# w_ada's forty later tiles, 2.85 units apart in the context's first mixer

## The chip, the cores and the metric

The kernel runs on one core of one Trainium2 chip, in fp32 throughout. The metric is the device time in microseconds, the median of several executions. The core has TensorE (PE), VectorE (DVE), ScalarE (ACT), GpSimd (POOL) and SyncE (SP), which here only issues loads. Each engine works through its own list in order and waits on semaphores.

## The reference, cut to what matters

Two layers work on 256 latent and 256 context tokens of width 1024. In each layer the modulation comes first:

```python
m = jax.nn.silu(cond) @ w + b          # cond: c and c_ctx, w = w_ada[l], 1024 x 6144
sh_a, sc_a, g_a, sh_f, sc_f, g_f = jnp.split(m, 6, axis=-1)
z = split_columns(modulate(x, norm1_gain[l], sh_a, sc_a) @ w_in[l])
mix = jnp.concatenate([pool_x, attn_x, ml_x], axis=-1) @ w_out[l]
x = x + g_a * mix
x = x + g_f * peer_ffn(modulate(x, norm2_gain[l], sh_f, sc_f), ...)
```

The context reads only itself; the latent tokens read themselves and the context. `pool_x` is a centred pooling, `attn_x` low-rank attention with 8 heads, `ml_x` a bidirectional matrix memory with 4 heads. `peer_ffn` picks 16 experts for each of 8 heads of each token out of 16384 and gathers their rows. The context's second layer ends after its keys, values and memory state.

## The kernel before, in words

The work has four mixers (`PHASES`): context layer 0, latent layer 0, context layer 1, latent layer 1. The first and the last run alone; the other two run behind the experts' gathers. This case lies in the first, `mixer(0)`, before any gather.

Each engine's list is written by Python generators that yield a time in units and are merged in order of it (`merge`). Among equal times the generator named first goes first, and the rest tiles' is named ahead of the mixer's. A unit is a place in the order, no duration. In the first mixer the input projection takes 3 units for each of its 16 groups from unit 12 on (`in_at`): 3, 3 and 2 matmuls. The memory stands at 45 (`ALONE_TIMES.ml`), the row products of keys and queries at 60, 64, 70 and 74, their transposes (row turns, L1675) 10 units later, the attention at 87 with 4 units for each of 8 steps, the out-projection at 129.

A step of the attention works on two heads: scores (L1692), VectorE's maxima, ScalarE's exponentials (L902), VectorE's shares, transposes of the probabilities (L1707), ScalarE's copies (L914) and the products with the values (L1722), which VectorE copies out (L1293).

Weights come in tiles of 128 x 2048 fp32 (1024 KB). For the first mixer there are 63 of them (`main_loads`): 8 `ada` tiles of w_ada's shift and scale for the first norm, which must come first; the forty `rest` tiles (16 left of layer 0, `REST_OF[0]`, and 24 of layer 1); 8 `in`, 1 `ukv`, 2 `uq`, 4 `out`. They are sorted by the unit of their first use and go in this order through a ring of five places (`ALONE`). In SyncE's list load n waits until load n - 5 is spent (`spent`: its last matmul done), and every later load stands behind it. An `in` tile serves two groups, 6 units; a `rest` tile is spent at once.

A rest tile (`ada_rest`) is 8 matmuls at L1499 with 32 columns of silu(c) as weights, at unit `rest_at(n)`. Its sum, in `bank[5]`, is copied by ScalarE to `modrow` (L709, unit `rest_at(n) + 1`), and ahead of the next tile TensorE turns it with two small matmuls (L1483, `turn`). After tile 15 VectorE builds `modT` and `A2` of layer 0 (L1048, L1051) at `rest_at(16) - 1`, and tile 16 waits for it; after tile 39 it does the same for layer 1 at `rest_at(40) + 1`. Layer 0's are read from the first out-projection on, layer 1's from the third mixer on.

Other lines that the prediction names: L1534 and L1528 are the input projection, L1506 sums of squares, L1544 and L1554 small transposes of the gates, L1739 the out-projection, L608 the loads of tiles.

Of the kernel before, what the change touches and what calls it, by code (L numbers as in the profile page):

```python
# [48 lines left out]
REST_OF = (ADA_TILES - ADA_FIRST, ADA_TILES)  # L49
# [59 lines left out]

def rest_at(n):  # L110

    return 13 + 2 * n if n < REST_OF[0] else 46 + 2.5 * (n - REST_OF[0])


def n2_at(p):
# [88 lines left out]
def main_loads():  # L204


    def mixer(p):
        at = BASE[p]
        uses = []
        for t in range(IN_TILES):  # L210
            own = [n for n, g in enumerate(groups(p)) if g[2] == t]
            if own:
                uses.append((p, "in", t, at + in_at(own[0]), at + in_at(own[-1]) + 2))
        for what, kinds in (("q", [("uq", 0), ("uq", 1)]), ("k", [("ukv", 0)])):
            rows = [at + row_at(p, j) for j, item in enumerate(items(p)) if item[1] == what]
            if rows:
                uses += [(p, kind, n, rows[0] + n, rows[1] + (n if kind == "uq" else 1)) for kind, n in kinds]
        if PHASES[p][2]:
            for b in range(OUT_TILES):
                first = at + TIMES[p].out + 2 * b * OUT_STEP  # L220
                uses.append((p, "out", b, first, first + OUT_STEP + 2))
        uses.sort(key=lambda u: u[3])
        return uses

    fast = [(0, "ada", j, j - 20, j - 20) for j in range(ADA_FIRST)]
    fast += [(0, "rest", n, rest_at(n), rest_at(n)) for n in range(REST)]
    fast = sorted(fast + mixer(0), key=lambda u: u[3])
    back = mixer(1) + mixer(2)
    last = mixer(3)
    return fast + last[BACK:], back + last[:BACK], len(fast)  # L230
# [91 lines left out]
def build(nc, x_in, c_in, par_in, con_in, w_in, wq_in, uq_in, pw_in, uv_tabs, out):  # L322
    with ExitStack() as ctx:
# [353 lines left out]
        def _(a):  # L677
# [25 lines left out]
            def rest_rows():  # L703
                for n in range(REST):
                    yield rest_at(n) + 1
                    a.wait_ge(rest_mm.sem, rest_mm.at(0, n + 1))
                    if n >= 2:
                        a.wait_ge(rest_tr.sem, rest_tr.at(0, n - 1))
                    a.activation(modrow[:, n % 2, :], bank[5][:, 0:WT], ACT.Copy).then_inc(rest_row.sem, 1)  # L709
# [325 lines left out]
        def _(v):  # L1035
# [21 lines left out]
            def first_scales():  # L1057
                yield 8.5
                v.wait_ge(ada_tr.sem, ada_tr.at(0, ADA_FIRST))
                modulation(0, 0, 16, bank[2], [mix_scale])  # L1060
                v.sem_inc(mod_ready.sem, 1)
                yield rest_at(REST_OF[0]) - 1
                v.wait_ge(rest_tr.sem, rest_tr.at(0, REST_OF[0]))
                modulation(0, 16, 48, bank[5][:, WT - 32:], [ff_scale])
                v.sem_inc(rest_scaled, 1)
                yield rest_at(REST) + 1
                v.wait_ge(rest_tr.sem, rest_tr.at(0, REST))
                modulation(1, 0, 48, bank[5][:, WT + 64:], [mix_scale, ff_scale])
                v.sem_inc(mod_ready.sem, 1)
# [897 lines left out]
```

## Time and profile before

| what | value |
|---|---|
| runs | 2668.5, 2670.63, 2673.1 us; median 2670.63 |
| the profiled execution's own time | span 2664.6 us from its first to its last instruction; no other total is recorded for it |
| TensorE busy | 2150.9 us, 81% of the span |
| VectorE, ScalarE, GpSimd busy | 1636.1, 1140.6, 810.0 us |
| mean granted TensorE clock | 0.949 |
| DMA | 940.05 MB, mean 353 GB/s |
| chain that ended last | DMA 45%, PE 33%, DVE 10%, ACT 7%, issue 3% |
| first mixer's out-projection begins | 251.45 us |

A busy share is an average over stages with different limits. From about 340 us on gathers fill the DMA engines for most of the span; the first mixer lies ahead of that, so it must be read by itself, in windows and in the timeline. In the timeline an fp32 matmul has two records, so "x16" is eight matmuls.

### The profile page before, as it was taken

What the parts mean: (1) busy time and instruction counts of PE and PEld (TensorE: products, weight loads), DVE (VectorE), ACT (ScalarE), POOL (GpSimd) and SP (SyncE); (2) the same over time, 40 slices, a digit from 0 to 9 for tenths busy, and PEclk for the clock granted to TensorE, in tenths of its full rate; (3) what the DMA queues carried; (4) which work ended last, traced back from release to release, by engine and by line L of the source; (5) the groups of instructions that cost most, each with busy time, mean ns of one, the idle gap of its engine ahead of it and who ended that gap; (6) DMA issues with size and microseconds to landing.
All of it is one profiled execution on the core that took longest, in us unless ns stands there. A gap on an engine that the chain in (4) does not pass through costs nothing.

```text
span 2664.6 us, 26635 instructions
## 1 busy us (share of the span) xinstructions
PE 2150.9 (81%) x8372; PEld 1003.3 (38%) x8372; DVE 1636.1 (61%) x4029; ACT 1140.6 (43%) x3280; POOL 810.0 (30%) x772
## 2 busy tenths in 40 slices
PE   6899889876788677796677777789989987777776
PEld 3667745432344243351122111166774321221111
DVE  1125376687887665766677666445536666677654
ACT  3144264555774434455333333335423333443332
POOL 0000033443445334333434333200004444343331
PEclk8999999978999889998899999999899999999999
DMA  7667199999999999999999999922019999999997
GB/s 302 255 247 316 34 397 412 396 362 392 407 399 405 421 414 412 418 419 421 422 421 422 421 422 421 412 89 76 36 34 392 425 426 426 425 426 426 426 426 308
DMA packets 133660, 940.05 MB, mean 353 GB/s; under 512 B 14864, under 2 KB 16144, under 8 KB 23312
## 3 DMA queue, kind: packets, MB, share of 16 engines
q0 software_dynamic: 110592, 805.36, 73.0%
q1 hardware_dynamic: 22496, 130.31, 12.4%
q10 hardware_dynamic: 432, 2.70, 0.3%
q8 instruction: 66, 1.08, 0.2%
q14 instruction: 74, 0.61, 0.1%
HBM read 937.26 MB, written 1.05 MB: 352 GB/s over the span
## 4 chain that ended last, share of the span: by engine, by line
DMA 45%; PE 33%; DVE 10%; ACT 7%; issue 3%; POOL 1%; SPq 0%; DVEq 0%; POOLq 0%; ACTq 0%
DMA fast<-uv_dram,idx 27%; DMA mix<-uv_dram,idx 14%; PE bank L1816 11%; PE bank L1775 5%; PE bank L1534 4%; DVE fast L1400 4%; PE bank L1739 2%; DMA qring<-wq_dram 2%; DMA fast<-w_dram 2%; PE bank L1499 2%; PE bank L1528 1%; PE bank L1784 1%; ACT diag L973 1%; ACT coef L970 1%; PE bank L1506 1%
## 5 line engine op out<-in xcount | busy, mean ns | idle before, releaser
L1816 PE MATMUL bank<-fast,diag 128*64 128x512 f32 x1956 | 797.0, 653 | 247.4 <-ACT diag L973 242.5
L667 POOL DMA_INDIRECT fast<-uv_dram,idx x489 | 525.8, 1075 | 1395.0 <-PE bank L1816 695.1
L1400 DVE SCALAR_TENSOR_TENSOR fast<-fast,hrow 128x1024 f32<-128x1024 f32 x489 | 598.3, 1224 | 347.9 <-DMA fast<-uv_dram,idx 342.2
L969 ACT ACTIVATE gact<-araw 128x1 f32<-128x1 f32 x768 | 154.5, 201 | 904.3 <-DVE fast L1400 548.2
L1816 PE MATMUL bank<-mix,diag 128*64 128x512 f32 x816 | 387.4, 628 | 99.3 <-ACT diag L973 96.5
L1816 PEld LDWEIGHTS bank<-fast,diag 128*64 128x64 f32 x1956 | 190.5, 144 | 706.6 <-ACT diag L973 454.3
L1400 DVE SCALAR_TENSOR_TENSOR mix<-mix,hrow 128x1024 f32<-128x1024 f32 x204 | 250.0, 1226 | 178.3 <-DMA mix<-uv_dram,idx 174.0
L667 POOL DMA_INDIRECT mix<-uv_dram,idx x204 | 203.4, 997 | 291.7 <-PE bank L1816 270.2
L973 ACT ACTIVATE diag<-con,coef 128x64 f32<-128x64 f32 x768 | 267.1, 348 | 25.1
L970 ACT ACTIVATE coef<-gact,wts 128x1 f32<-128x1 f32 x768 | 226.2, 295 | 24.9
L1816 PEld LDWEIGHTS bank<-mix,diag 128*64 128x64 f32 x816 | 93.2, 139 | 341.2 <-ACT diag L973 224.7
L1775 PE MATMUL bank<-hT,qring 128*128 128x256 f32 x640 | 192.0, 421 | 32.7 <-DMA qring<-wq_dram 24.0
L1775 PEld LDWEIGHTS bank<-hT,qring 128*128 128x128 f32 x640 | 115.0, 199 | 145.9 <-issue 103.6
L1816 PE MATMUL bank<-hT,diag 128*64 128x512 f32 x224 | 114.7, 637 | 41.0 <-ACT diag L973 40.3
L1400 DVE SCALAR_TENSOR_TENSOR hT<-hT,hrow 128x1024 f32<-128x1024 f32 x56 | 68.6, 1224 | 41.2 <-DMA hT<-uv_dram,idx 41.2
L1534 PE MATMUL bank<-hT,back 128*128 128x256 f32 (+1 forms) x336 | 84.1, 390 | 4.0 <-ACT hT L716 4.0
L667 POOL DMA_INDIRECT hT<-uv_dram,idx x56 | 56.6, 1011 | 95.5 <-PE bank L1816 92.8
L1534 PE MATMUL bank<-hT,fast 128*128 128x256 f32 (+1 forms) x320 | 81.3, 407 | 4.8 <-ACT hT L716 4.8
L1816 PEld LDWEIGHTS bank<-hT,diag 128*64 128x64 f32 x224 | 27.3, 142 | 115.7 <-ACT diag L973 76.6
L1534 PEld LDWEIGHTS bank<-hT,fast 128*128 128x128 f32 (+1 forms) x320 | 62.1, 200 | 22.7 <-issue 13.2
L1534 PEld LDWEIGHTS bank<-hT,back 128*128 128x128 f32 (+1 forms) x336 | 63.4, 191 | 18.0 <-issue 7.4
L969 ACT ACT_TABLE_LOAD x53 | 68.0, 1283 | 0.9
(265 smaller groups left out, 2588.6 us busy)
## 6 DMA issues: line engine op xcount, KB each, us to landing
fast<-w_dram SPq DMA_DIRECT2D x72, 1024.0 KB, 8.9
qring<-wq_dram SPq DMA_DIRECT2D x40, 576.0 KB
back<-w_dram SPq DMA_DIRECT2D x20, 1024.0 KB
fast<-uv_dram,idx POOLq DMA_INDIRECT x489
mix<-wq_dram SPq DMA_DIRECT2D x8, 576.0 KB, 5.6
mix<-uv_dram,idx POOLq DMA_INDIRECT x204, 27.5
fast<-uq_dram SPq DMA_DIRECT2D x4, 576.0 KB, 3.8
xT<-x_dram ACTq DMA_DIRECT2D x1, 2048.0 KB, 8.6
```

The source lines that it names most:

```text
L667: g.indirect_dma_start(slot(e, m), None, uv_tabs[e], bass.IndirectOffsetOnAxis(idx[:, Q % 2, n:n + 1], 0)).then_inc(landed[place], 16)
L969: link(a.activation(gact[:, n:n + 1], araw[:, Q % 2, n:n + 1], ACT.Gelu))
L970: link(a.activation(coef[:, n:n + 1], gact[:, n:n + 1], ACT.Copy, scale=wts[:, Q % 2, n:n + 1]))
L973: a.activation(diag[:, m % DIAGS, :], two, ACT.Copy, scale=coef[:, n:n + 1]).then_inc(diag_ready.sem, 1)
L1400: v.scalar_tensor_tensor(out=u, in0=u, scalar=1.0, in1=hrow[:, (2 * i + half) % 3, :], op0=ALU.mult, op1=ALU.mult, accum_out=araw[:, Q % 2 ...
L1499: mm = t_.matmul(bank[5][strip(k), 0:WT], cS[:, k, :], w[:, k, :], start=(k < STRIPS), stop=(k >= KC - STRIPS))
L1506: t_.matmul(bank[3][:, 0:SEQ], ones, sq[:, n % 2, :], start=first, stop=last).then_inc(sq_used.sem, 1)
L1528: mm = t_.matmul(bank[g % 2][:, 0:WT], own_h(p)[:, k, n * P:(n + 1) * P], w[:, k, :], start=(k == 0), stop=(k == KC - 1))
L1534: mm = t_.matmul(bank[g % 2][0:rows, 0:SEQ], w[:, k, o:o + rows], own_h(p)[:, k, :], start=(k == 0), stop=(k == KC - 1))
L1739: mm = t_.matmul(bank[b % 2][:, 0:SEQ], w[:, k, b % 2 * P:b % 2 * P + P], own_h(p)[:, k, :], start=(k == 0), stop=(k == KC - 1))
L1775: mm = t_.matmul(dst[:, 0:SEQ], query_tile(e, u)[:, k, :], own_h(p)[:, k, :], start=(k == 0), stop=(k == KC - 1))
L1816: mm = t_.matmul(acc[half, f * 512:(f + 1) * 512], diag[:, j % DIAGS, :], slot(e, j)[:, D + f * 512:D + (f + 1) * 512], start=(j % SLOTS < ...
```

## The change

The spacing of the forty rest tiles is one line. Before, tiles 0 to 15 stood at units 13 to 43, 2 apart, and tiles 16 to 39 at units 46 to 103.5, 2.5 apart. Now all stand 2.85 apart, from 13 to 124.15. What hangs on `rest_at` moves along: copies, turns, VectorE's two modulations (from unit 45 to 57.6 and from 107 to 128), and the place of each tile in the order of loads. No instruction is added or removed.

```diff
 def rest_at(n):
 
-    return 13 + 2 * n if n < REST_OF[0] else 46 + 2.5 * (n - REST_OF[0])
+    return 13 + 2.85 * n
```

The order of loads around the in tiles, as tile (unit of first use), from load 8 on:

before: in 0 (12), rest 0 (13), 1 (15), 2 (17), in 1 (18), rest 3 (19), 4 (21), 5 (23), in 2 (24), rest 6 (25), 7 (27), 8 (29), in 3 (30), rest 9 (31), 10 (33), 11 (35), in 6 (36), rest 12 (37), 13 (39), 14 (41), in 5 (42), rest 15 (43)

now: in 0 (12), rest 0 (13), 1 (15.85), in 1 (18), rest 2 (18.7), 3 (21.55), in 2 (24), rest 4 (24.4), 5 (27.25), in 3 (30), rest 6 (30.1), 7 (32.95), 8 (35.8), in 6 (36), rest 9 (38.65), 10 (41.5), in 5 (42), rest 11 (44.35), 12 (47.2), in 4 (48), rest 13 (50.05)

First place: SyncE's list, from the loads that wait for an ada tile on. `in_mm` is the semaphore of a spent in tile, `rest_mm` of a spent rest tile, `ada_mm` of a spent ada tile. Before:

```order
L608 DMA fast<-w_dram 128x2048 [waits ada_mm] x8
L608 DMA fast<-w_dram 128x2048 [waits in_mm]
L608 DMA fast<-w_dram 128x2048 [waits rest_mm] x3
L608 DMA fast<-w_dram 128x2048 [waits in_mm]
L608 DMA fast<-w_dram 128x2048 [waits rest_mm] x3
L608 DMA fast<-w_dram 128x2048 [waits in_mm]
```

Now:

```order
L608 DMA fast<-w_dram 128x2048 [waits ada_mm] x8
L608 DMA fast<-w_dram 128x2048 [waits in_mm]
L608 DMA fast<-w_dram 128x2048 [waits rest_mm] x2
L608 DMA fast<-w_dram 128x2048 [waits in_mm]
L608 DMA fast<-w_dram 128x2048 [waits rest_mm] x2
L608 DMA fast<-w_dram 128x2048 [waits in_mm]
```

Three loads that wait for rest tiles stood between two that wait for an in tile; now two do here (three once, later).

Second place: TensorE's list from the second or third rest tile on, beside in tiles 0 and 1 and the start of in tile 2. Before:

```order
L1499 MATMUL bank<-fast,cS 32x256 x8
L1534 MATMUL bank<-hT,fast 128x256 x2
L1544 MATMUL bank<-con,mix 128x32 x2
L1534 MATMUL bank<-hT,fast 128x256 x3
L1483 MATMUL bank<-con,keysA 128x2 x2
L1499 MATMUL bank<-fast,cS 32x256 x8
L1534 MATMUL bank<-hT,fast 128x256 x5
L1483 MATMUL bank<-con,keysA 128x2 x2
L1499 MATMUL bank<-fast,cS 32x256 x8
L1534 MATMUL bank<-hT,fast 128x256 x6
L1483 MATMUL bank<-con,keysA 128x2 x2
L1499 MATMUL bank<-fast,cS 32x256 x8
```

Now:

```order
L1499 MATMUL bank<-fast,cS 32x256 x8
L1534 MATMUL bank<-hT,fast 128x256 x8
L1483 MATMUL bank<-con,keysA 128x2 x2
L1499 MATMUL bank<-fast,cS 32x256 x8
L1534 MATMUL bank<-hT,fast 128x256 x8
L1506 MATMUL bank<-mix,con 128x256 x2
L1483 MATMUL bank<-con,keysA 128x2 x2
L1499 MATMUL bank<-fast,cS 32x256 x8
```

Between two tiles (L1499) stood 5 or 6 projection matmuls (L1534); now 8 do.

Third place: TensorE's list from the last two steps of the attention to the out-projection (L1739). Before:

```order
L1722 MATMUL bank<-hrow,mix 64x128 x2
L1707 MATMUL bank<-con,hrow 128x128 x2
L1722 MATMUL bank<-hrow,mix 64x128 x2
L1707 MATMUL bank<-con,hrow 128x128 x2
L1722 MATMUL bank<-hrow,mix 64x128 x2
L1707 MATMUL bank<-con,hrow 128x128 x2
L1722 MATMUL bank<-hrow,mix 64x128 x4
L1739 MATMUL bank<-hT,fast 128x256 x19
```

Now:

```order
L1483 MATMUL bank<-con,keysA 128x2 x2
L1499 MATMUL bank<-fast,cS 32x256 x8
L1707 MATMUL bank<-con,hrow 128x128 x2
L1722 MATMUL bank<-hrow,mix 64x128 x4
L1483 MATMUL bank<-con,keysA 128x2 x2
L1499 MATMUL bank<-fast,cS 32x256 x8
L1483 MATMUL bank<-con,keysA 128x2 x2
L1739 MATMUL bank<-hT,fast 128x256 x19
```

Rest tiles with their turns now stand between the last transposes, and the last turn directly ahead of the out-projection.

## Rows read from the trace of the kernel before

**Rows 1.** Waits of TensorE, 0 to 300: us in total, times, longest us.
```profile
PE bank L1499 <- DMA fast<-w_dram: 15.3, 5, 3.5
```

**Rows 2.** Waits of the load queue, 0 to 300: us in total, times, longest us.
```profile
SPq L608 <- PE bank L1534: 86.6, 6, 18.6
```

**Rows 3.** Chain of waits, 55 to 135: start us, us, what.
```profile
58.29 4.83 DMA fast<-w_dram
...
91.51 4.76 DMA fast<-w_dram
...
124.55 5.01 DMA fast<-w_dram
```

**Rows 4.** TensorE's timeline: start, us, operation, records, in brackets idle before.
```profile
63.17 1.94 PE L1499 MATMUL bank<-fast,cS 128*32 128x256 f32 x16 [2.84 <-DMA fast<-w_dram]
65.03 4.48 PE L1534 MATMUL bank<-hT,fast 128*128 128x256 f32 x10
...
80.99 1.07 PE L1499 MATMUL bank<-fast,cS 128*32 128x256 f32 x16 [2.44 <-DMA fast<-w_dram]
...
86.22 2.86 PE L1534 MATMUL bank<-hT,fast 128*128 128x256 f32 x12
88.92 0.50 PE L1483 MATMUL bank<-con,keysA 128*128 128x2 f32 x4
89.35 1.07 PE L1499 MATMUL bank<-fast,cS 128*32 128x256 f32 x16
90.35 2.43 PE L1534 MATMUL bank<-hT,fast 128*128 128x256 f32 x10
...
96.32 1.77 PE L1499 MATMUL bank<-fast,cS 128*32 128x256 f32 x16 [3.20 <-DMA fast<-w_dram]
98.02 3.37 PE L1534 MATMUL bank<-hT,fast 128*128 128x256 f32 x10
...
112.92 1.32 PE L1499 MATMUL bank<-fast,cS 128*32 128x256 f32 x16 [3.38 <-DMA fast<-w_dram]
114.18 3.81 PE L1534 MATMUL bank<-hT,fast 128*128 128x256 f32 x10
...
129.61 1.07 PE L1499 MATMUL bank<-fast,cS 128*32 128x256 f32 x16 [3.45 <-DMA fast<-w_dram]
130.61 4.11 PE L1528 MATMUL bank<-fast,hT 128*128 128x256 f32 x10
```

**Rows 5.** Windows: stretch, busy us of each engine (records), clock, DMA share, GB/s.
```profile
62.50:69.50 7.00, 6.33 (x29) 4.20 (x29) 2.21 (x6) 0.38 (x1) 0.00 (x0) 0.52 1.02 430
...
134.50:212.00 77.50, 76.75 (x553) 51.68 (x552) 27.20 (x51) 40.58 (x83) 0.00 (x0) 0.98 0.69 272
```

**Rows 6.** Timelines of TensorE (204.16, 209.16) and VectorE (201.38), row phase.
```profile
204.16 1.08 PE L1675 MATMUL bank<-con,hrow 128*96 128x128 f32 x8
...
209.16 1.94 PE L1499 MATMUL bank<-fast,cS 128*32 128x256 f32 x16
...
201.38 0.96 DVE L1253 TENSOR_TENSOR hrow<-hrow,par 128x768 f32<-128x768 f32 x1
```

**Rows 7.** TensorE's timeline, attention to out-projection.
```profile
222.97 1.13 PE L1692 MATMUL bank<-mix,fast 96*128 96x256 f32 x4
...
229.96 1.16 PE L1692 MATMUL bank<-mix,fast 96*128 96x256 f32 x4 [0.91 <-ACT hrow L902]
...
238.36 0.61 PE L1483 MATMUL bank<-con,keysA 128*128 128x2 f32 x4 [0.17 <-ACT keysA L709]
...
239.75 1.13 PE L1692 MATMUL bank<-mix,fast 96*128 96x256 f32 x4
...
242.65 1.13 PE L1692 MATMUL bank<-mix,fast 96*128 96x256 f32 x4
...
251.45 4.80 PE L1739 MATMUL bank<-hT,fast 128*128 128x256 f32 x21 [0.38 <-DVE hT L1293]
```

**Rows 8.** Groups by line, 0 to 300: busy us, mean ns, idle before.
```profile
L709 ACT ACTIVATE keysA<-bank 128x256 f32<-128x256 f32 x40 | 15.3, 382 | 64.9 <-PE bank L1499 64.7
```

## The prediction

> **What bounds the kernel now.** I read the waits of TensorE and of the load queue first, over the stretch that the change touches (the start to 300 us). TensorE waits 15.3 us in five pieces for weight tiles at L1499, the matmuls of w_ada's later tiles [rows 1]. The load queue's largest wait is 86.6 us, for L1534, the in-projection [rows 2]: a load stands still until a projection tile is spent, and all loads behind it stand too. The chain of waits shows each case as one piece, "DMA fast<-w_dram": there are five, of 4.76 to 5.01 us from issue to landing, and every one begins in the moment an in-projection tile is spent [rows 3]. The timeline of TensorE then shows what a wait costs: the idle time in brackets, and slower matmuls behind it [rows 4]. The table of windows shows the granted clock and the transfer rate after the first wait, and that from 134.5 to 212 us TensorE is busy 76.75 of 77.5 us [rows 5]. So this mixer is bound by TensorE, except for five holes in which it waits for a tile.
>
> Why the holes are there. The five places of the ring are refilled in order of use, so the load of number n waits for number n-5. An in tile is held for 6 units. With rest tiles 2 units apart, three stand between two in tiles, and the tile that reuses an in tile's place is a rest tile due 2 units after the in tile is spent: rest 3 after in 0 (19 against 17), rest 6 after in 1 (25 against 23), rest 9 after in 2, rest 12 after in 3, rest 15 after in 6. In 2 units TensorE has under 2.5 us of work, and the load takes 4.8. That gives exactly the five waits of the trace. After rest 16 the distance of 2.5 units gives no sixth.
>
> **The change part by part.** Nothing is added or removed: 40 tiles, each with 8 matmuls, a turn of 2 matmuls, a copy on ScalarE and a load of 1 MB. Units of work at full clock, from [rows 4]: six projection matmuls take 88.92 - 86.22 = 2.70 us, so 0.45 each; a turn (L1483) 89.35 - 88.92 = 0.43; a tile 90.35 - 89.35 = 1.00. (A matmul is two records.)
>
> First, the five idle stretches. They are 2.84, 2.44, 3.20, 3.38 and 3.45 us, sum 15.3. With 2.85 units between rest tiles, the tile that reuses an in tile's place comes later. The work between the last matmul on the in tile and the wait for the new one becomes:
> in 0 to rest 3: 3 matmuls, turn and tile, 8 matmuls, turn: 11 x 0.45 + 1.43 + 0.43 = 6.8 us;
> in 1 to rest 5: the same 6.8 us and the two small groups L1506 and L1554;
> in 2 to rest 7: 8 matmuls, turn and tile, turn: 3.60 + 1.43 + 0.43 = 5.46 us;
> in 3 to rest 9: 5.46 us;
> in 6 to rest 12: 16 matmuls, two tiles with turns, turn: 7.2 + 2.86 + 0.43 = 10.5 us.
> Loads land 4.76 to 5.01 us after issue when nothing is queued ahead [rows 3]. A tile of 1.05 MB takes 1.05 / 0.43 = 2.44 us of transfer at the 430 GB/s of [rows 5]. Each of the first releases sends out three loads, of which the third lands after 4.8 + 2 x 2.44 = 9.7 us, and the next release comes after 16 matmuls and two tiles with turns, 7.2 + 2.86 = 10.1 us: nothing is queued ahead of the next burst. Only ahead of rest 12 is one more load, and there 10.5 us are free. The places of the later in tiles, of ukv and of uq are wanted again 4 units and more after their release, as from rest 16 on before, where nothing waited. So all five waits go: -15.3 us, with 0.45 us to spare at two places.
>
> Here the Trainium skill speaks against the change: "DMA: Bandwidth & Descriptors", section Specifications, gives about 358 GB/s as a core's limit from HBM. By it a tile takes 2.93 us, a load about 5.3, and the two tight places would have 0.15 us left. The trace does not agree: it shows 430 GB/s.
>
> Second, the clock behind the holes. The stretch from 62.5 to 69.5 has a granted clock of 0.52 [rows 5], so half of it and more ran at 1.2 GHz where full is 2.4. Row by row against the full-speed row (five projection matmuls in 2.43, a tile in 1.07) [rows 4]: first wait 4.48 - 2.43 = 2.05 and 1.94 - 1.07 = 0.87; second nothing; third 0.94 and 0.70; fourth 1.38 and 0.25; fifth 1.68. Sum 7.9 us. I take all of it back, since each slow piece follows an idle stretch of 2.8 us or more and no other piece between 48 and 134 is slow. Bounds: 0, if the clock falls without a wait too, as at 209.16, where a tile took 1.94 us with no idle time in front [rows 6]; and 7.9 + 0.9 = 8.8, if that one goes as well.
> By the Trainium skill, "TensorE: Matmul & The Clock Gate", section HAM oscillation, it is waits for DMA between bursts that bring the half rate again and again. By that rule alone the whole 7.9 would come back; the row at 209.16 does not agree with it as the only cause.
>
> Third, the moved tiles. Before, rest 0 to 32 (33 tiles) stand ahead of the attention (unit 87); after, rest 0 to 25. Seven tiles go behind the fourth step's scores (unit 99): -7 x 1.43 = -10.0 us there, +10.0 us here, if TensorE is the bound at both ends. Ahead, what the other engines must deliver stays in time: the closest is the row turn at 204.16, whose rows VectorE finished at 201.38 + 0.96 = 202.34 [rows 6], 1.8 us early, and two tiles stand between its last row product and it before and after alike. In the attention, a step without a tile is 242.65 - 239.75 = 2.90 us [rows 7]; the small waits between scores, turns and values in it can take up a little of a tile. The step from 222.97 to 229.96 lasts 6.99 us with two tiles, 2.90 + 2.86 = 5.76 of it work: there VectorE and ScalarE hold TensorE, but this place has three tiles around it before and after. I take 7 x 0.1 = 0.7 us of gain (bounds 0 and 1.5). At the end the last tile and its turn now stand right ahead of the out-projection, and the turn waits for ScalarE's copy, 0.38 us [rows 8] and a hand-over each way, 0.6 us; in exchange the 0.38 us wait at 251.45 [rows 7] is covered: +0.2 us. VectorE's modulation for layer 1 moves there as well and is needed only in the latent tokens' later phase; the out tiles' loads follow rest 35 to 38 and have over 5 us before their use.
>
> Sum: -15.3 - 7.9 - 0.7 + 0.2 = -23.7 us. All that follows (queries, gathers, later mixers) starts when this mixer ends and has no other clock, so it moves as a whole. Against the profiled span: 2664.6 - 23.7 = 2640.9. The median of the runs shown is 6.0 us over that span, so 2670.6 - 23.7 = 2646.9 us.
>
> **The rivals.**
> A, the two tight places still wait. For: 0.45 us to spare is little, and loads spread by 0.25 us. Against: every landing of the trace is below 5.1. Price from the nearest case, one more tile queued ahead: 4.8 + 2.44 - 5.46 = 1.8 us each, and with it a slow piece of 7.9 / 5 = 1.6 each: 6.8 us less gain, 2653.7 us.
> B, the clock falls anyway. For: the row at 209.16. Against: the long stretch 134.5 to 212 is at 0.98 with no waits. The 7.9 us stay: 2654.8 us.
> C, the change only shifts the holes: the load that reuses an in tile's place is late whatever the distance, and five waits stay. Against: rest 18, 20 and 22 of before, 4 and more units behind their release, wait for nothing. 2670.6 us.
> D, slower: the attention cannot take the tiles. Nine tiles now stand between unit 99 and 129, each with a turn that waits for ScalarE, whose copy may stand behind an exponential that waits for VectorE. If each of the nine waited out a whole step of 2.90 us, that is 26.1 us against the 23.7 gained: 2673.0 us, slower; it decides from 2.6 us a tile. Against: the turn at 238.36, the only one that waited, did so for 0.17 us [rows 7].
>
> **How the numbers follow.** My forecast 0.64, A 0.14, B 0.12, C 0.05, D 0.05. A and B together would be 2661. The range leaves out about 2 in 10: it goes from 2641 (the slow piece at 209 gone, the attention at its best, and 3 us of scatter as the three runs have) to 2658 (A or B with scatter). No change means within 0.2%, 5.3 us, about what a measurement of this kernel can tell. Faster: forecast, A, B and a little of C, 0.91; same 0.05; slower 0.04.
>
> **What would show it.** The waits for "DMA fast<-w_dram" at L1499 between 50 and 135 us gone, or under 1 us in sum; the out-projection's first matmul at about 228 in place of 251.45; granted clock near 1.0 in the stretch from 50 to 110; the tile's matmuls in every step of the attention, steps of 4.3 us and more where they were 2.9; one wait of some 0.6 us ahead of L1739. Two waits of 1 to 2 us would be A, projection rows of 3 to 4 us with no idle time ahead B. A wait of over 1 us at L1483 in the attention would make me wrong in D's direction.

## The result and the profile after

The changed kernel takes 2653.11 us (median of 4 runs, 2651.11 to 2655.41) against 2671.56 us (median of 4 runs on the same chip, 2668.5 to 2673.1): a ratio of 0.9928, 95% interval 0.9915 to 0.9941. That is 18.5 us less, where 23.7 were forecast. A second timing of the same code, below as e_same, gives 0.9916 (0.9903 to 0.9928), 23.2 us less than its own runs of before. The two intervals overlap, and a gain of some 21 us (a ratio of 0.992) lies within both; I take it as the size.

First the waits of TensorE from 0 to 300 us, after (us in total, times, longest us), to be read against [rows 1].

```profile
PE bank L1473 <- DMA fast<-w_dram: 15.3, 2, 14.7
PE bank L1534 <- ACT hT L716: 4.8, 1, 4.8
...
PE bank L1692 <- ACT fast L888: 1.2, 1, 1.2
...
PE bank L1692 <- ACT hrow L902: 0.9, 1, 0.9
...
PE bank L1483 <- ACT keysA L709: 0.7, 2, 0.5
```

The row of L1499, five times and 15.3 us, is gone. The waits at L1473 at the kernel's start are 15.3 us in all, where they were 16.3. New is one of 1.2 us at the first scores (L1692) for ScalarE's L888, the copy of the last row turn.

The load queue's waits, after, in the same columns, against [rows 2]:

```profile
SPq L608 <- PE bank L1534: 64.2, 6, 17.3
SPq L608 <- PE bank L1499: 54.1, 21, 4.5
```

The queue still stands most of the time: loads go out when places come free, and now most of them are freed by later tiles instead of projection tiles. That costs nothing, since TensorE waits for none of it.

TensorE's timeline after, on the stretch that answers to the first wait of [rows 4] (start us, us, operation, records, in brackets the idle time before):

```profile
60.40 1.07 PE L1499 MATMUL bank<-fast,cS 128*32 128x256 f32 x16
61.40 3.72 PE L1534 MATMUL bank<-hT,fast 128*128 128x256 f32 x16
64.95 0.50 PE L1483 MATMUL bank<-con,keysA 128*128 128x2 f32 x4
65.39 1.07 PE L1499 MATMUL bank<-fast,cS 128*32 128x256 f32 x16
```

No brackets, a tile in 1.07 us and sixteen projection records in 3.72: all at full rate. Two windows after (stretch, busy us of PE, PEld, DVE, ACT, POOL with records, granted clock, DMA share, GB/s), and the same two before:

```profile
46.00:130.00 84.00, 83.40 (x582) 63.51 (x586) 20.03 (x47) 27.95 (x60) 0.00 (x0) 0.97 0.65 253
150.00:229.00 79.00, 76.14 (x663) 50.81 (x662) 39.95 (x112) 42.32 (x110) 0.00 (x0) 1.00 0.85 319
```

```profile
46.00:130.00 84.00, 68.68 (x483) 50.04 (x485) 15.92 (x37) 20.89 (x46) 0.00 (x0) 0.90 0.56 220
150.00:229.00 79.00, 78.15 (x610) 52.81 (x608) 33.42 (x73) 44.84 (x96) 0.00 (x0) 0.98 0.78 315
```

In the first 84 us TensorE is now busy 83.40 instead of 68.68 and the clock is 0.97 instead of 0.90. Last, the attention and the out-projection after, against [rows 7]:

```profile
181.49 1.10 PE L1692 MATMUL bank<-mix,fast 96*128 96x256 f32 x4 [1.17 <-ACT fast L888]
...
202.11 1.13 PE L1692 MATMUL bank<-mix,fast 96*128 96x256 f32 x4
...
206.46 1.13 PE L1692 MATMUL bank<-mix,fast 96*128 96x256 f32 x4
...
210.04 0.61 PE L1483 MATMUL bank<-con,keysA 128*128 128x2 f32 x4 [0.17 <-ACT keysA L709]
...
228.90 0.61 PE L1483 MATMUL bank<-con,keysA 128*128 128x2 f32 x4 [0.50 <-ACT keysA L709]
229.37 2.84 PE L1739 MATMUL bank<-hT,fast 128*128 128x256 f32 x12
```

A step of the attention with a tile lasts 206.46 - 202.11 = 4.35 us, the 2.90 + 1.43 of the working. The out-projection starts at 229.37, 22.1 us earlier than at 251.45.

Where the profiled spans' difference of 15.3 us (2664.6 to 2649.3) lies, from the first row of each operation in the two timelines:

| stretch | before | after | difference |
|---|---|---|---|
| start to the first in-projection (L1534) | 45.2 | 46.6 | +1.4 |
| from there to the first scores (L1692) | 168.9 | 134.9 | -34.0 |
| scores to out-projection (L1739) | 37.3 | 47.9 | +10.6 |
| queries, gathers, mixers 1 and 2, layer 0's experts, to the last expert product at 1737.9 and 1716.0 | 1486.4 | 1486.6 | +0.2 |
| to layer 1's first query (1956.64 and 1940.26) | 218.8 | 224.3 | +5.5 |
| to the end | 708.0 | 709.0 | +1.0 |

The first mixer is 23.4 us shorter. The lead is still 21.9 us at 1716.0, and then the last mixer, which the change doesn't touch, gives back 5.5.

### The profile page after: what moved, and what is told of

Same layout as the page of the kernel before. It is cut to its first block, busy times and chain, and to the rows that moved or that the text cites. A ratio compares the mean times of both kernels' runs of the same rounds, so it can differ in the third digit from the quotient of the medians.

```text
span 2649.3 us, 26635 instructions
## 1 busy us (share of the span) xinstructions
PE 2151.9 (81%) x8372; PEld 1004.5 (38%) x8372; DVE 1636.5 (62%) x4029; ACT 1138.7 (43%) x3280; POOL 814.6 (31%) x772
## 3 DMA queue, kind: packets, MB, share of 16 engines
q8 instruction: 66, 1.08, 0.2%
## 4 chain that ended last, share of the span: by engine, by line
DMA 44%; PE 34%; DVE 9%; ACT 7%; issue 3%; POOL 1%; another core or an unknown queue 0%; SPq 0%; DVEq 0%; POOLq 0%; ACTq 0%
DMA fast<-uv_dram,idx 26%; DMA mix<-uv_dram,idx 15%; PE bank L1816 11%; PE bank L1775 4%; PE bank L1534 4%; DVE fast L1400 3%; PE bank L1739 2%; DMA qring<-wq_dram 2%; PE bank L1528 1%; PE bank L1499 1%; PE bank L1784 1%; ACT diag L973 1%; ACT coef L970 1%; PE bank L1506 1%; PE bank L1623 1%
## 5 line engine op out<-in xcount | busy, mean ns | idle before, releaser
L1775 PE MATMUL bank<-hT,qring 128*128 128x256 f32 x640 | 192.8, 423 | 35.0 <-DMA qring<-wq_dram 23.7
L1534 PE MATMUL bank<-hT,back 128*128 128x256 f32 (+1 forms) x336 | 84.5, 391 | 4.0 <-ACT hT L716 4.0
L1534 PE MATMUL bank<-hT,fast 128*128 128x256 f32 (+1 forms) x320 | 75.7, 390 | 4.8 <-ACT hT L716 4.8
L939 ACT ACTIVATE pq<-bank 128x256 f32<-128x256 f32 x48 | 18.2, 380 | 125.6 <-PE bank L1775 116.1
L1534 PEld LDWEIGHTS bank<-hT,back 128*128 128x128 f32 (+1 forms) x336 | 63.9, 192 | 18.3 <-issue 7.4
```

Source lines behind the costliest of these rows:

```text
L1534: mm = t_.matmul(bank[g % 2][0:rows, 0:SEQ], w[:, k, o:o + rows], own_h(p)[:, k, :], start=(k == 0), stop=(k == KC - 1))
L1775: mm = t_.matmul(dst[:, 0:SEQ], query_tile(e, u)[:, k, :], own_h(p)[:, k, :], start=(k == 0), stop=(k == KC - 1))
```

## The experiments

Unless said otherwise, each kernel is the changed one with the one line in rest_at changed. The 40 tiles are numbered n = 0 to 39, and REST_OF[0] is 16. "Out" is the start of the first L1739.

**e_same, the change again.**

```
+    return 13 + 2.85 * n
```

> The changed kernel once more, to see what of its result repeats. Both profiles so far agree that the first mixer's out-projection begins 22 us earlier (251.45 to 229.37) and that layer 0's last expert product starts 21.9 us earlier; 6.2 us of it are lost in the last mixer, between 1738 and 2000 us, whose code is untouched and whose granted clock was lower. Theory (scatter of the clock): the first mixer repeats within 2 us, the last mixer comes out anywhere between 258 and 270 us, and the time is 16 to 22 us under before. Rival (the change itself slows the last mixer): its length is again 268 to 270 us.

Measured: 2650.25 us (5 runs) against 2673.43 (20 runs); ratio 0.9916 (0.9903 to 0.9928); out at 229.58. These 20 runs of before also serve the next three. From the first in-projection to the out-projection it takes 182.9 us, after 182.8, so the first mixer repeats. The stretch of the last mixer that took 218.8 us before and 224.3 after takes 221.2 us here: between the two, as scatter would have it. The gain of 23.2 us is a little over the 16 to 22 expected.

**e_late_only, only the later 24 tiles spread.**

```
-    return 13 + 2.85 * n
+    return 13 + 2 * n if n < REST_OF[0] else 46 + 3.25 * (n - REST_OF[0])
```

> Tiles 0 to 15 stay 2 units apart, tiles 16 to 39 stand 3.25 apart up to 120.75: the move of tiles into the attention without the wider spacing in front. Theory (ring waits): the five waits for w_dram at L1499 stay, 14 to 16 us in sum, the out-projection begins at 251 +-2, time within 0.2% of before. Rival (the gain comes from moving tiles out of the stretch ahead of the attention into its gaps): no less than 8 us faster.

Measured: 2672.96 us (12 runs), ratio 1.0 (0.9991 to 1.001), out at 251.84. Its waits of TensorE, 0 to 300 us:

```profile
PE bank L1499 <- DMA fast<-w_dram: 15.3, 5, 3.3
```

The five waits are untouched, and tiles moved from ahead of the attention into it gain nothing by themselves: the stretch to the scores is 6.4 us shorter (162.5), the attention 6.3 longer (43.6). So the gain hangs on the first sixteen.

**e_front_only, the first sixteen at 2.85, the rest squeezed to end about where they did.**

```
-    return 13 + 2.85 * n
+    return 13 + 2.85 * n if n < REST_OF[0] else 58.6 + 1.975 * (n - REST_OF[0])
```

> Tiles 0 to 15 stand 2.85 apart, tiles 16 to 39 closer, 1.975 apart, so that the last stands before unit 106 as in the kernel before. Theory: all five waits are gone, no new wait of over 1 us for w_dram, out-projection at 228 to 231, time 16 to 22 us under before, like the whole change. Rival (moved tiles): under half of the change's gain, 10 us or less.

Measured: 2660.24 us (9 runs), ratio 0.9953 (0.9938 to 0.9968), out only at 248.22. The expectation missed. The waits of TensorE, 0 to 300 us, are few:

```profile
PE bank L1483 <- ACT keysA L709: 3.1, 4, 1.5
PE bank L1499 <- DMA fast<-w_dram: 2.7, 2, 1.9
```

Together they are 5.8 us, yet the out-projection is 18.8 us behind that of after. (The profiled execution, span 2663.6, was a slower one than the median; the runs put the loss against e_same at 10 us.) The timeline shows half-rate rows in two kinds of place:

```profile
158.58 1.93 PE L1499 MATMUL bank<-fast,cS 128*32 128x256 f32 x16 [1.88 <-DMA fast<-w_dram]
...
191.79 1.94 PE L1675 MATMUL bank<-con,hrow 128*96 128x128 f32 x8
```

The first stands right behind waits of 0.53 and 1.88 us, the second has only one of 0.79 us ahead of it, over 3 us earlier. The windows show what they cost, here of e_front_only (columns as above):

```profile
160.00:180.00 20.00, 20.00 (x116) 12.03 (x108) 6.77 (x13) 9.91 (x19) 0.00 (x0) 0.81 0.55 220
180.00:200.00 20.00, 18.60 (x159) 12.22 (x158) 7.05 (x13) 9.34 (x20) 0.00 (x0) 0.79 1.01 412
200.00:228.00 28.00, 26.46 (x190) 17.95 (x193) 13.24 (x41) 11.86 (x33) 0.00 (x0) 0.73 0.82 303
```

and of after:

```profile
160.00:180.00 20.00, 20.00 (x170) 13.85 (x168) 9.19 (x16) 12.90 (x26) 0.00 (x0) 1.00 0.86 338
180.00:200.00 20.00, 17.83 (x170) 12.42 (x162) 13.94 (x43) 12.18 (x33) 0.00 (x0) 1.00 0.94 364
200.00:228.00 28.00, 27.81 (x262) 18.24 (x264) 10.73 (x43) 11.07 (x40) 0.00 (x0) 1.00 0.83 292
```

From 160 to 180 both are busy for the whole 20 us, but one finishes 170 records and the other 116, at a clock of 0.81. From 180 to 200 the changed kernel idles more (2.17 against 1.40 us) and keeps the full clock. So more idle time is not what costs here; the clock is. The expectation had nothing for it.

**e_two_waits, the first seven tiles still 2 units apart.**

```
-    return 13 + 2.85 * n
+    return 13 + 2 * n if n < 7 else 25 + 2.85 * (n - 6)
```

> Tiles 0 to 6 stand 2 apart, all others 2.85: of the five places where a load waits for an in tile, the first two keep their distance of 2 units. Theory: exactly two waits for w_dram at L1499 stay, at tiles 3 and 6, 4.8 to 5.5 us in sum, with the slow matmuls behind them (2.9 us by the rows of before), so the out-projection begins some 8 us later than in the changed kernel, at 236 to 239, and the time is about 11 us under before. Rival (any wider mean spacing brings the gain, the single place does not matter): as fast as the changed kernel within 2 us.

Measured: 2656.8 us (6 runs), ratio 0.9947 (0.9934 to 0.9961), out at 236.99. Its timeline of TensorE has two waits for tiles:

```profile
64.48 1.56 PE L1499 MATMUL bank<-fast,cS 128*32 128x256 f32 x16 [2.87 <-DMA fast<-w_dram]
80.99 1.07 PE L1499 MATMUL bank<-fast,cS 128*32 128x256 f32 x16 [2.41 <-DMA fast<-w_dram]
```

Two waits of 5.3 us are back, and behind each a slow piece: tile and projection behind the first take 1.6 us more than at full rate, the projection and a small transpose behind the second 1.6 too. The out-projection comes 7.4 us later than in e_same and the kernel takes 6.6 us more. But this profile's in-projection began 1.35 us earlier (45.36 and 46.71), ahead of anything that differs; counted from there the out-projection comes 8.8 us later, 5.3 for the waits and 3.2 for the clock behind them, close to the 4.8 to 5.5 and the 2.9 expected. Waits come back singly, exactly where a place of the ring is wanted too early.

**e_one_wait, tiles 17 and 18 earlier by 2.6 and 4.3 units.** It asks whether a wait alone brings the slow clock of e_front_only.

```
-    return 13 + 2.85 * n
+    return {17: 58.9, 18: 60.01}.get(n, 13 + 2.85 * n)
```

> The changed kernel, but tiles 17 and 18 stand at units 58.9 and 60.01 instead of 61.45 and 64.3, so that tile 18, whose load waits for in 7 (spent at 59), is wanted one unit later. It asks why the run with only the front tiles spread lost 16 us with just 2.7 us of waits for tiles: its granted clock fell to half in three stretches after 158 us. Theory W (one wait of 1 to 2 us at this place, between small matmuls, brings the slow stretches): a wait of 1 to 1.5 us at tile 18 near 141 us, slow stretches of 10 us and more behind it in the first mixer, the out-projection 5 us or more later than the changed kernel's 229.4. Theory D (tiles close together in the stretch of row products and turns, units 60 to 106, bring it: 24 there against 16): the same wait, and the out-projection at 231 to 233, no slow stretch after 60 us.

Measured: 2650.81 us (6 runs) against 2671.64 (11 runs, which serve this and the next three), ratio 0.9928 (0.9909 to 0.9947), out at 230.03. The row of TensorE's timeline:

```profile
145.78 1.07 PE L1499 MATMUL bank<-fast,cS 128*32 128x256 f32 x16 [1.25 <-DMA fast<-w_dram]
```

A wait of 1.25 us, and the tile behind it at full rate; the clock stays at 1.00 in every window from 140 to 228. Counted from the first in-projection the out-projection comes 1.6 us later than in e_same, for this wait and 0.7 us of others at the turns (L1483): no clock was lost. The wait is shorter than the 0.53 and 1.88 us ahead of the first slow piece of e_front_only, so it leaves open what brought that piece.

**e_uniform_26, all tiles 2.6 units apart.**

```
-    return 13 + 2.85 * n
+    return 13 + 2.6 * n
```

> All tiles 2.6 apart, the last at unit 114.4. By the arithmetic of the ring no load is late (the closest has the same 5.5 us as in the changed kernel), so by the theory that only the waits count it is as fast as the changed kernel: no wait over 0.5 us for w_dram, 18 to 24 us under before. The turn that stood bare ahead of the out-projection is covered, 0.5 us. If tile density costs clock (theory D), 18 tiles stand in units 60 to 106 against 16, and a slow stretch of 3.4 us may be there, 1.7 us. Rival: the value 2.85 itself matters, and 2.6 is over 5 us slower.

Measured: 2652.69 us (6 runs), ratio 0.9931 (0.991 to 0.9951), out at 229.12: no difference from the change that can be told. One wait for a tile is there, 0.96 us at 106.63, where none over 0.5 was expected: between release and use lie 5.3 us, and this load took 6.22 from issue to landing (100.36 to 106.58 in the chain of waits). So a place with half a us to spare can fail; why this landing was late isn't shown. Another wait is of 1.54 us for ScalarE's copy at 198.83, and behind it a tile and a scores row run at half rate, 1.6 us lost. So 2.85 is not a special number.

**e_early_two and e_early_three, the first two or three tiles ahead of the in-projection.** TensorE waits 4.8 us there for hT in all other kernels; these fill the hole.

```
-    return 13 + 2.85 * n
+    return 8.1 + 0.1 * n if n < 2 else 13 + 2.85 * (n - 1)
...
-                    yield rest_at(n) + 1
+                    yield rest_at(n) + (0.5 if n < 2 else 1)
```

(and with 3 and n - 2 in the other)

> Tiles 0 and 1 move to units 8.1 and 8.2, ahead of the input projection, where TensorE of both kernels waits 4.8 us for the normed rows; their copies move to 0.5 behind, ahead of the modulation on ScalarE; all later tiles keep 2.85 and end 2.85 units earlier. Theory: two tiles with turns, 2.9 us, go into the 4.8 us wait, which falls to about 1.5 us with the hand-overs to ScalarE, and with less idle time the slow stretch behind it (44.3 to 51.1 us in the changed kernel, 3.4 us of cost) may go. 2.9 to 6 us faster than the changed kernel, out-projection at 223 to 227. Rival: the copies on ScalarE delay the modulation, and it is no faster.

> The same with three tiles at 8.1 to 8.3. Each takes 1.0 us of matmuls, some 0.6 for the copy and hand-overs and 0.4 for its turn, so three are 6 us against the 4.8 us wait. Theory: the third gains at most its turn and tile (1.4 us) and delays the modulation on ScalarE by up to 1.3 us: within 1.5 us of the kernel with two. Rival (TensorE's work alone counts): 1.4 us faster than with two.

Measured: e_early_two 2643.85 us (6 runs), ratio 0.9904 (0.9887 to 0.992), out at 226.22; e_early_three 2648.28 (6 runs), 0.9914 (0.9898 to 0.993). TensorE's timeline after, at the start of the in-projection:

```profile
46.60 2.85 PE L1534 MATMUL bank<-hT,fast 128*96 128x256 f32 x6 [4.79 <-ACT hT L716]
49.38 1.70 PE L1499 MATMUL bank<-fast,cS 128*32 128x256 f32 x16
```

and that of e_early_two, from the end of the work ahead of it:

```profile
41.67 1.07 PE L1499 MATMUL bank<-fast,cS 128*32 128x256 f32 x16
43.25 0.61 PE L1483 MATMUL bank<-con,keysA 128*128 128x2 f32 x4 [0.50 <-ACT keysA L709]
43.78 1.81 PE L1499 MATMUL bank<-fast,cS 128*32 128x256 f32 x16
46.65 7.01 PE L1534 MATMUL bank<-hT,fast 128*96 128x256 f32 x22 [1.06 <-ACT hT L716]
```

The in-projection starts at the same time, and two tiles are done by then. Out comes 3.2 us earlier than after, as expected; the slow stretch at the start of the projection, which might have gone, stays (clock 0.83 from 40 to 60 in both). It has the lowest median of all, 6.4 us under e_same and 7.0 under e_one_wait; the intervals of the ratios overlap, so that it beats the change by time is likely rather than shown, that it beats before is shown. The third tile starts the projection 0.9 us later (47.51) and adds a turn that waits 0.50 us: out comes 0.2 us earlier than with two, no further gain to speak of. Its median is 4.4 us above that of e_early_two, more than the 1.5 expected; the first mixer doesn't show them, and the intervals overlap.

**e_dense, as the change up to tile 21, the rest 1.7 units apart.** It asks for the slow clock of e_front_only without a wait for a tile.

```
-    return 13 + 2.85 * n
+    return 13 + 2.85 * n if n < 22 else 75.7 + 1.7 * (n - 22)
```

> Tiles 0 to 21 as in the changed kernel, tiles 22 to 39 stand 1.7 apart from unit 75.7 to 104.6, behind the last projection weights, so that many tiles stand between small matmuls but no load has to be late. 23 tiles stand in units 60 to 106, as many as in the run with only the front tiles spread (23), against 18 in the kernel before and 16 in the changed one. Theory D (density of tiles, whose matmuls have 32 columns of weights, between row turns and memory products brings the low clock): one or more slow stretches between 165 and 225 us, 10 us or more in sum, out-projection at 235 or later, 5 us or more slower than the changed kernel. Theory W (it was the wait for a tile): waits for w_dram under 0.5 us, clock 1.0, out-projection at 229 to 231.

Measured: 2662.04 us (5 runs) against 2671.89 (9 runs), ratio 0.9965 (0.9952 to 0.9979), out at 237.47, 8 us later than the change. Its windows (columns as above), and its timeline of TensorE:

```profile
140.00:165.00 25.00, 25.00 (x166) 14.88 (x166) 13.75 (x23) 15.44 (x34) 0.00 (x0) 1.00 0.74 296
165.00:200.00 35.00, 34.50 (x338) 23.92 (x340) 16.35 (x42) 19.25 (x44) 0.00 (x0) 0.95 0.98 401
200.00:237.00 37.00, 34.33 (x226) 21.97 (x218) 15.55 (x57) 14.48 (x47) 0.00 (x0) 0.77 0.73 278
```

```profile
177.71 0.61 PE L1483 MATMUL bank<-con,keysA 128*128 128x2 f32 x4
178.25 1.65 PE L1499 MATMUL bank<-fast,cS 128*32 128x256 f32 x16
179.82 1.94 PE L1675 MATMUL bank<-con,hrow 128*96 128x128 f32 x8
...
203.21 1.02 PE L1483 MATMUL bank<-con,keysA 128*128 128x2 f32 x4 [2.48 <-ACT keysA L709]
204.16 1.93 PE L1499 MATMUL bank<-fast,cS 128*32 128x256 f32 x16
206.02 0.69 PE L1707 MATMUL bank<-con,hrow 128*128 128x128 f32 x2
206.64 1.12 PE L1722 MATMUL bank<-hrow,mix 128*64 128x128 f32 x4
207.68 2.08 PE L1692 MATMUL bank<-mix,fast 96*128 96x256 f32 x4
```

No wait for a tile is left, and the half clock is there: from the tile at 178.25 on, with no idle time in front since 140 (25.00 of 25 us busy; of the next 35 only 0.50 are idle, at 183.79, behind it), and from about 203 for some 17 us. The first piece costs 1.7 us. This second piece stands behind a wait of 2.48 us, so for it, the larger one, density and wait are not told apart.

**e_before_again and e_before_third, the kernel before, profiled twice more.** They ask whether the 5.5 us lost in the last mixer belong to the change.

> The kernel before once more, for the last mixer: from layer 0's last expert product to layer 1's first query it took 218.8 us in the profile of before, 220.1 to 225.1 us in nine profiles of kernels with other rest tiles, whose code there is the same. Theory (scatter): 219 to 225 here too, and out-projection of the first mixer at 251 to 252. Rival (the spread of the rest tiles costs something in the last mixer): 217 to 220.

> The same once more, a third profile of the kernel before, with the same two expectations: 219 to 225 us by scatter, 217 to 220 if the spread tiles cost something there.

Measured: one run each, 2674.7 and 2677.46 us, spans 2672.9 and 2675.7. The last mixer from layer 0's last expert product to the first query, as windows of the first profile of before, of e_before_again, and of after:

```profile
1737.90:1956.60 218.70, 198.47 (x948) 154.79 (x946) 98.98 (x231) 94.69 (x198) 0.00 (x0) 0.93 0.17 60
```

```profile
1738.60:1963.60 225.00, 203.62 (x948) 158.50 (x946) 99.49 (x231) 94.82 (x198) 0.00 (x0) 0.90 0.16 58
```

```profile
1716.00:1940.30 224.30, 202.92 (x949) 157.91 (x947) 99.58 (x231) 94.88 (x198) 0.00 (x0) 0.90 0.16 59
```

The same 948 records take 198.47 us at a clock of 0.93 or 203.62 at 0.90, in one and the same kernel. Over the 13 profiles of this study the stretch lasts 218.8 to 225.1 us, and the shortest is that of the first profile of before, the one that the prediction was read from. So the last mixer came out as scatter would have it (225.0 and 224.7 us). The first did not: its out-projection begins at 252.8 and 248.6, where 251 to 252 were expected.

## Why the prediction was right, and where its sizes were off

The forecast was 2647 us with a range of 2641 to 2658; the time is 2653.11, and 2650.25 in the second timing. The mechanism held: the five waits and the slow rows behind them were the cost, and both are gone. One step did not hold, that the other engines deliver in time ahead of the attention, and three sizes were off.

*The five idle stretches, -15.3.* Right. All five are gone, also at the places with 0.45 us to spare, ahead of tiles 7 and 9, which start at 81.76 and 90.45 without a bracket. Rival A (two tight places still wait) and C (the holes only shift) fall with that, though A's fear had a ground: in e_uniform_26 a load took 6.22 us and was waited for. e_two_waits puts two waits back by position alone, and e_late_only all five, with no gain left: the waits are shown as the source.

*The clock behind the holes, -7.9.* Right in kind, sized too low. To the scores the stretch is 34.0 us shorter. Summed from start to start in the two timelines, idle time falls by 13.9 us (the five waits of 15.3 gone, 1.2 us new at the first scores and 0.2 elsewhere), tiles and turns by 12.7, projection rows by 6.5 and row turns by 0.7. Seven tiles moved away are some 10.4 of the 12.7, so 9.5 us are left for the clock, above the upper bound of 8.8. The bound counted 0.9 us for the slow piece at 209.16 and left out its second row:

```profile
211.02 1.82 PE L1675 MATMUL bank<-con,hrow 128*96 128x128 f32 x8
```

At full rate that row takes 1.08 us [rows 6], so the piece cost 1.6 us. It is gone as well: the clock is 1.00 from 150 to 229. Rival B (the clock falls anyway) falls for this kernel. But its ground was sound: in e_dense the half clock at 179.82 has no idle time in front. Nor is the clock's price fixed: in e_before_third the same five waits (14.7 us) cost 6.4 us of slow rows where they cost 7.9, behind the last, of 3.15 us, all rows are at full rate, and nothing is slow near 209. Of the kernels with the later tiles 2.85 or 3.25 units apart, none has a slow piece between 150 and 226; at 2.6 and 2.5 units there is one of some 3 us (at 199.36 in e_uniform_26, 209.16 in before) in all but that one profile of before; at 1.975 and 1.7 it is about 20 us or more. So the slow pieces go with the close spacing, in four kernels; which feature of it brings them no run tells.

*The moved tiles, -0.7.* Here a step failed: "what the other engines must deliver stays in time". At 181.49 the first scores wait 1.17 us for ScalarE's L888, and the chain of waits after (start us, us, what) shows what held ScalarE:

```profile
177.38 1.28 ACT L823
...
179.09 1.29 ACT mix L823 x3
180.41 0.35 issue
180.77 0.59 ACT fast L888
```

A table load and four of the memory's exponentials (L823) stand ahead of the copy; before, ScalarE had done them and waited 0.61 us for TensorE (at 212.15). The wait is there in every kernel with the later tiles 2.85 or 3.25 apart, and in none of the closer ones. In the attention itself there was no gain either: it took 10.6 us more, where 10.0 less 0.7 and the 0.2 of the last turn make 9.5. By the same sums seven tiles are 7.1 of it and their turns 3.7, 0.52 us each among the small products where 0.43 were reckoned; idle time was 1.5 us before and 1.6 after, so the steps had no holes for tiles to fill.

What I undersold is the spacing of the later tiles. By my sum their move was worth 0.7 us; e_front_only, without it, lost 10 us against e_same (2660.24 to 2650.25), mostly to the clock. Still, that kernel squeezes them to 1.975 units, below the 2.5 of before; no run has the first tiles spread and the later ones at 2.5, and e_uniform_26, with 2.6 throughout, lost nothing that can be told.

*The last turn, +0.2.* Right: 0.50 us of wait at 228.90 in place of the 0.38 at 251.45. Rival D (the attention can't take the tiles) falls: the turns in it wait 0.17 us in all up to that last one.

*"All that follows moves as a whole."* Right for the work in this pair: 22.08 us of lead at the first products with the experts' keys (L1784, 331.68 to 309.60) and 21.9 at 1716.0. The last mixer's clock then hid 5.5 us of it, and the repeats show that this is scatter. The stretch between scatters too: from the out-projection to the last expert product e_before_third took 7.0 us more than before.

*The sum* of the first mixer came out to 0.3 us (-23.4 for -23.7), and that is in part luck: 1.6 us too little for the clock stood against 1.2 us for the new wait and 1.1 for the attention. The out-projection's lead is only 22.1 us, as the in-projection began 1.4 us later in this profile.

*The frame* was "the median of the runs shown is 6.0 us over that span". In every run with both figures the time is about 1.8 us over its span (2651.11 and 2649.3), so by my estimate the profiled execution took about 2666.4, 4.2 us under that median: a short one. Repeats of the same kernel have spans of 2672.9 and 2675.7, 8 and 11 us more. Out-projection starts of the changed kernel at 229.37 and 229.58 against 251.45, 252.8 and 248.6 of the three profiles of before give a lead of 19 to 23 us, 21.5 in the mean. The gains of 18.5 and 23.2 us by the medians lie on both sides of that; 23.7 was a little high.

Left open: how much of the half clock behind 203 in e_dense its one wait of 2.48 us brings, what besides the close spacing a slow piece without idle time needs, and whether e_early_two is faster than the change by more than its intervals tell.

## What to carry to other kernels

In a ring of loads that is refilled in order, write for each load which place it waits for, and compare the work between that place's release and the new tile's use with one landing (here 4.8 us, once 6.2): here the places that fell short cost their idle time and about half as much again in clock. Even spacing over the whole stage cured it; closing up the tiles in one part to spread them in another brought the half clock back, in part without any wait. An engine that sped-up work now catches up with must be looked at too: here ScalarE, 1.2 us. Before a sum is set against a profiled span, look how far repeated profiles of the same kernel lie apart, here 11 us of 2665.

## What the runs showed of the hardware

- The granted clock can fall to half without idle time in front. In e_dense TensorE was busy 25.00 of 25 and 34.50 of 35 us when the row at 179.82 took 1.94 us instead of 1.08 [rows 6]. Waits of 0.96 and 1.25 us (e_uniform_26, e_one_wait) had full-speed rows behind them, one of 1.54 us (e_uniform_26, 198.83) half-rate rows, and of those of 2.4 us and more most had half-rate rows, but not the last of e_before_third (3.15 us).
- An untouched stretch of 948 records took 218.8 to 225.1 us in 13 profiles, with mean clocks from 0.93 to 0.90 in the five profiles where it was read.
- One core's DMA moved 412 GB/s over 20 us (180 to 200 in e_front_only). The Trainium skill, "DMA: Bandwidth & Descriptors", section Specifications, has about 358 GB/s as a core's limit; the trace does not agree with it.
